# Scores and probability transposes of an attention group moved inside the next unit's projection, in a float32 two-block transformer kernel

## The chip, the cores and the metric

The kernel runs on one core of a Trainium2 chip. The metric is the device time of one execution in microseconds (us), lower is better. A profiled execution is one execution recorded by the hardware profiler; its trace gives for every instruction the engine, the start and the duration. TensorE is PE in the rows (PEld are its weight loads), VectorE is DVE, ScalarE is ACT, GpSimd is POOL, SyncE is SP.

## The reference

One sequence of 256 tokens by 1024 channels goes through two blocks in float32. The first is two layers: a multi-scale pooling mixer, and a differential attention of 8 heads, each followed by a gated feed-forward (1024 to 2816). The second is a token mixer with three branches (a block attention of 8 heads, a top-64 attention of 8 heads, a gated recurrence), followed by a squared-ReLU feed-forward (1024 to 4096). The attention parts, cut to what matters here:

```python
# differential attention, per head: two score maps of one head
s = einsum(q, k) * sm_scale + bias            # causal
p = softmax(s)
a = p[:, :, 0] - lam * p[:, :, 1]
o = einsum(a, v)

# the two attentions of the second block, per pair of heads
logits = einsum(q, k) * scale + bias (+ mask of the keys not chosen, second attention)
out = softmax(logits) @ v
```

## The kernel before

**Weights stream in units.** All weight matrices are cut into units of 128 x 2048 numbers (512 KB twice over). A unit is loaded by SP into one of three `raw` buffers, rounded by ScalarE into `w_hi` (line 1178, two instructions of 128x1024), and VectorE puts the rest, raw minus rounded, into `w_lo` (line 1190, two instructions). A product is then three fast matmuls: `w_hi` with the rounded activation, `w_hi` with the activation's rest, `w_lo` with the rounded activation (`three`, all recorded at line 525). A projection of one unit (`project`) is two column blocks of 8 such triples, 48 matmuls of 256 columns.

**The order is written out by hand.** Each engine has its own program, and semaphores link them. The units of the attention parts are: `U_HEAD` to `U_HEAD+7` (query and key of head 0 to 7, attention steps 0 to 7), `U_MOBA` to `U_MOBA+3` (steps 8 to 11, `A_MOBA` is 8), and `U_DSA` to `U_DSA+3` (steps 12 to 15, `A_DSA` is 12). These are the three attention groups. Two units `U_XC` follow the second group and two `U_YC` the third. A table of turns (`HEAD_TURNS`, `TURNS`) gives to each unit the step that is scored in its turn and the step that is applied in it: the step scored belongs to the unit before, the step applied to the unit two before. So in a group's second unit the group's first step is scored and nothing is applied; in its third unit the second step is scored and the first applied.

**One turn on TensorE, before:** `pe_turn_probs` (the transposes of the probabilities of the step that is applied, line 875; 3 in the first group, 6 in the others), then `pe_score` (the scores of the step that is scored: 4 float32 matmuls, recorded as 8), then the unit's projection, then `pe_apply` (the product with the values). `pe_score` waits for `proj_copied`: ScalarE must have copied the unit before from its PSUM bank into `qk` (line 1353). A unit's projection goes to bank 4, or to bank 5 where the unit is in `BANK5`.

**One turn on the others, first group** (loop over `HEAD_TURNS`): VectorE copies the transposed probabilities to SBUF (`v_prob_t`, line 1999, waits for `turned`), makes the logits (`v_logits`, line 1805, waits for `scored`), makes the rest of the unit two further on (`v_split`, line 1190), scales the exponentials to probabilities (`v_probs`, lines 1813 to 1822), and copies the output. ScalarE rounds the unit two further on, takes the exponentials (`s_softmax`, line 1318), copies the projected unit (line 1353), and sums squares.

**One turn on the others, second and third group** (`s_mixer`, `v_mixer`): here ScalarE begins the turn with the copy of the transposed probabilities (line 1373, waits for `turned`), and then rounds the unit two further on (line 1178), takes the exponentials (line 1318) and copies the projected unit (line 1353). VectorE makes logits (line 1805; in the third group with a mask added first, line 1798), the rest (line 1190), the probabilities (lines 1813, 1818), and then a piece of top-k or of a convolution and the rest of the output.

Of the kernel before, what the change touches and what calls it, by code (L numbers as in the profile page):

```python
# [25 lines left out]
KT = D // P  # L26
# [35 lines left out]
SLOTS = 3  # L62
# [6 lines left out]
U_HEAD = U_V + 4  # L69
# [3 lines left out]
U_QI = U_VA + 2  # L73
U_KI = U_QI + 2
U_VB = U_KI + 1
U_MOBA = U_VB + 2
U_XC = U_MOBA + 4
U_DSA = U_XC + 2
# [7 lines left out]
A_MOBA, A_DSA, A_END = 8, 12, 16  # L86
# [17 lines left out]
    return hi_place(unit)  # L104


BANK5 = (U_HEAD + 1, U_QI + 1, U_MOBA + 1)


def step_of(unit):  # L110
# [84 lines left out]
def build(nc, t, out):  # L195
    with ExitStack() as ctx:
# [3 lines left out]
        def sem(name):  # L200
            return ctx.enter_context(nc.semaphore(name))
# [11 lines left out]
        far_hi, far_lo = x_far[:, :, 0:SEQ], x_far[:, :, SEQ:2 * SEQ]  # L213
# [77 lines left out]
        lo_done = sem("lo_done")  # L291
        unit_done = sem("unit_done")
# [55 lines left out]
        v_copied = sem("v_copied")  # L348
# [9 lines left out]
        o_copied = sem("o_copied")  # L358
# [41 lines left out]
        def part(tile, slot, a):  # L400
            return tile[slot][:, :].rearrange("p (a b) -> p a b", a=a)
# [125 lines left out]
        def three(out_, w, w_rest, a, a_rest, start, stop):  # L527

            mm(out_, w, a, start=start, stop=False)
            mm(out_, w, a_rest, start=False, stop=False)  # L530
            return mm(out_, w_rest, a, start=False, stop=stop)
# [8 lines left out]
        def lo_part(slot, place, a):  # L540
            return lo_cells[slot][:, place:place + UW].rearrange("p (a b) -> p a b", a=a)

        def project(slot, outs, hi, lo, nk=KT, place=0):

            whi, wlo = part(w_hi, slot, nk), lo_part(slot, place, nk)
            for j, o in enumerate(outs):
                for k in range(nk):
                    c = slice(j * P, (j + 1) * P)
                    last = three(o, whi[:, k, c], wlo[:, k, c], hi[:, k, :], lo[:, k, :], k == 0, k == nk - 1)
            return last  # L550
# [305 lines left out]
        def proj_out(unit):  # L856
            return two5 if unit in BANK5 else two4

        def project_free(eng, unit):

            before = COPIED[unit] - (unit - 1 in BANK5)
            if before and unit not in BANK5:
                eng.wait_ge(proj_copied, before)

        def pe_turn_probs(eng, a):

            eng.wait_ge(prob_ready, a + 1)
            if 1 <= a <= A_MOBA:
                eng.wait_ge(pt_copied, a)
            elif a > A_MOBA:  # L870
                eng.wait_ge(pt_copied2, a - A_MOBA)
            for m in range(1 if a < A_MOBA else 2):
                for b in range(3):
                    c = slice(b * P, (b + 1) * P)
                    last = nc.tensor.transpose(bank[6 + m][:, c], prob[:, m, c], ident[:, :])  # L875
            last.then_inc(turned, 1)

        def pe_score(eng, a, unit):
            eng.wait_ge(proj_copied, COPIED[unit] + 1)
            if a >= 2:  # L880
                eng.wait_ge(logits_read, a - 1)
            if a == A_MOBA:
                eng.wait_ge(v_copied, 3)
                eng.wait_ge(dots_relu, 8)
            q_k = qk[a % 2]
            for m in range(2):
                s, r = bank[2 * (a % 2) + m], slice(m * DH, (m + 1) * DH)
                mm(s[:, 0:P], q_k[r, 0, 0:P], q_k[r, 1, 0:P], start=True, stop=True)
                last = mm(s[:, P:384], q_k[r, 0, P:SEQ], q_k[r, 1, 0:SEQ], start=True, stop=True)
            last.then_inc(scored, 1)  # L890

        def pe_apply(eng, a):
            if a < A_MOBA:
                eng.wait_ge(pt_copied, a + 1)
            else:
                eng.wait_ge(pt_copied2, a - A_MOBA + 1)
            if a >= 1:
                eng.wait_ge(o_copied, a)
            if a < A_MOBA:
                h = slice(a * VD, (a + 1) * VD)  # L900
                mm(bank[5][:, 0:P], prob_t[:, 0, 0:P], v1[:, 0, h], start=True, stop=True)
                mm(bank[5][:, P:SEQ], prob_t[:, 0, P:SEQ], v1[:, 0, h], start=True, stop=False)
                last = mm(bank[5][:, P:SEQ], prob_t[:, 0, SEQ:384], v1[:, 1, h], start=False, stop=True)
            else:
                v = v_a if a < A_DSA else v_b
                for m in range(2):
                    hd = 2 * ((a - A_MOBA) % 4) + m
                    o, h = bank[5][m * DH:(m + 1) * DH, :], slice(hd * DH, (hd + 1) * DH)
                    mm(o[:, 0:SEQ], v[:, 0, h], prob_t[:, m, 0:SEQ], start=True, stop=False)
                    last = mm(o[:, P:SEQ], v[:, 1, h], prob_t[:, m, SEQ:384], start=False, stop=True)  # L910
            last.then_inc(applied, 1)
# [45 lines left out]
        def pe_mixer(eng):  # L957
            score_unit = {step_of(u): u for u in range(U_QI, U_GATE)}
            for unit, apply, score_step in TURNS[2:]:
                if apply is not None:  # L960
                    pe_turn_probs(eng, apply)
                if score_step is not None:
                    pe_score(eng, score_step, score_unit[score_step])
                eng.wait_ge(lo_done, unit + 1)
                s = unit % SLOTS
                if unit in COPIED:
                    project_free(eng, unit)
                if unit == U_KI:
                    whi, wlo = (w[s][:, 0:KI_COLS * KT].rearrange("p (k c) -> p k c", k=KT) for w in (w_hi, w_lo))
                    for k in range(KT):  # L970
                        last = three(bank[4][0:KI_COLS, 0:SEQ], whi[:, k, :], wlo[:, k, :], far_hi[:, k, :],
                                     far_lo[:, k, :], k == 0, k == KT - 1)
                elif U_VB <= unit < U_MOBA:
                    j = unit - U_VB
                    if j == 0:
                        eng.wait_ge(v_copied, 2)
                    for i in range(NT):
                        last = rows(both_parts(unit, 4), [[bank[0][:, :]], [bank[1][:, :]]], far_hi, far_lo, 4 * j, 4, 512, j == 0, j == 1,
                                    (i,))
                        if i == 1:  # L980
                            last.then_inc(unit_done, 1)
                        if (i, j) == (0, 0):
                            eng.wait_ge(proj_copied, COPIED[U_KI] + 1)
                            for n in range(NT):
                                last = nc.tensor.transpose(bank[5][:, IDX_HEADS * n:IDX_HEADS * (n + 1)],
                                                           wi_t[:, n * P:(n + 1) * P], ident[DH:KI_COLS, DH:KI_COLS])
                            last.then_inc(wi_turned, 1)
                        pe_dots(eng, 2 * j + i)
                else:
                    last = project(s, proj_out(unit), far_hi, far_lo)  # L990
                if not U_VB <= unit < U_MOBA:
                    last.then_inc(unit_done, 1)
                if apply is not None:
                    pe_apply(eng, apply)
# [35 lines left out]
        def _(eng):  # L1030
# [79 lines left out]
                last.then_inc(psum_open, 1)  # L1110

            for unit, apply, score_step in HEAD_TURNS[:-1]:
                if apply is not None:
                    pe_turn_probs(eng, apply)
                if unit is None:
                    eng.wait_ge(x_ready, 4 * O_NORM + 1)
                    open_tile(0)
                if score_step is not None:
                    if score_step == 0:
                        eng.wait_ge(v_copied, 1)  # L1120
                    pe_score(eng, score_step, U_HEAD + score_step)
                if unit is not None:
                    eng.wait_ge(lo_done, unit + 1)
                    project_free(eng, unit)
                    project(unit % SLOTS, proj_out(unit), far_hi, far_lo).then_inc(unit_done, 1)
                if apply is not None:
                    pe_apply(eng, apply)
                if unit in (U_HEAD + 4, U_HEAD + 6):
                    pe_pair(eng, (unit - U_HEAD - 4) // 2)
# [206 lines left out]
        def s_copy_unit(eng, unit):  # L1336

            eng.wait_ge(unit_done, unit + 1)
            both = bank[5 if unit in BANK5 else 4][:, :].rearrange("p (a b) -> p a b", a=2)
            if unit == U_KI:  # L1340
# [883 lines left out]
```

## Time and profile before

| | us |
|---|---|
| three runs | 946.9, 947.38, 947.76 |
| median | 947.38 |
| the profiled execution | 947.05 |
| its span, first to last instruction | 945.2 |
| mean granted TensorE clock | 0.998 of full |

| engine | busy, us | share of the span |
|---|---|---|
| PE | 932.9 | 99% |
| PEld | 825.4 | 87% |
| DVE | 668.5 | 71% |
| ACT | 473.4 | 50% |
| POOL | 35.1 | 4% |

A busy time is the sum over instructions of one engine, overlaps counted once. The end of a matmul is modelled by the profiler, and matmuls overlap in the array; so the distance from one matmul's start to the next one's start tells what it costs, and the busy row tells only that TensorE hardly ever stands. The three attention groups lie at about 230 to 300, 547 to 591 and 591 to 636 us of the span.

### The profile page before, as it was taken

Reading aid. Unit: us, or ns where it says so; the run is one execution under the profiler, and the core shown is the slowest. Engines: PE = TensorE matmul, PEld = TensorE weight load, DVE = VectorE, ACT = ScalarE, POOL = GpSimd, SP = SyncE. Lnnn points to the kernel's source line nnn. Section 1 sums busy time; section 2 is a strip of 40 time slices with the busy share of each in tenths; the row PEclk is TensorE's granted clock in tenths of the full one; section 3 lists DMA queues with packets and bytes.
Section 4 is the critical chain, followed back from the end, with each engine's and each line's share of the span. In section 5 each row is a group of like instructions: output and inputs, shape, how many; then the busy total and the mean of one; then the engine's idle time right before and its main releaser. Section 6 shows DMA issues by size and latency. Waiting matters only on the chain.

```text
span 945.2 us, 15383 instructions
## 1 busy us (share of the span) xinstructions
PE 932.9 (99%) x5899; PEld 825.4 (87%) x5899; DVE 668.5 (71%) x964; ACT 473.4 (50%) x730; POOL 35.1 (4%) x63
## 2 busy tenths in 40 slices
PE   9999999999999999999999999999999999999997
PEld 7888888888898988888888889899999888888886
DVE  4776767676787887667678587976975666666663
ACT  4544444436666444444446556567754454434432
POOL 2010001000000000000001000000000000000000
PEclk9999999999999999999999999999999999999999
DMA  8586666639533387656554845544665536555531
GB/s 297 196 280 233 199 222 212 209 134 267 173 128 103 111 262 245 215 189 206 194 178 123 246 138 131 159 134 138 212 207 184 206 121 215 205 183 192 205 136 45
DMA packets 141648, 175.67 MB, mean 186 GB/s; under 512 B 7152, under 2 KB 119985, under 8 KB 141598
## 3 DMA queue, kind: packets, MB, share of 16 engines
q1 hardware_dynamic: 138384, 166.55, 54.7%
q0 software_dynamic: 2656, 8.31, 2.6%
q8 instruction: 34, 0.56, 0.3%
q10 hardware_dynamic: 558, 0.12, 0.1%
q14 instruction: 16, 0.13, 0.0%
HBM read 173.88 MB, written 1.09 MB: 185 GB/s over the span
## 4 chain that ended last, share of the span: by engine, by line
PE 90%; DVE 5%; ACT 2%; issue 1%; DMA 1%; POOL 0%; DVEq 0%; POOLq 0%; SPq 0%; ACTq 0%
PE bank L525 88%; DVE w_lo L1190 1%; PE bank L875 1%; PE bank L661 1%; ACT w_hi L1178 1%; DMA raw<-w_up 1%; DVE stats L1613 0%; DVE x_rows L1628 0%; DVE x_rows L1621 0%; DVE x_both L1600 0%; DVE arena L2059 0%; PE bank L673 0%; ACT arena L1318 0%; POOL rstd L2121 0%; ACT bank L1235 0%
## 5 line engine op out<-in xcount | busy, mean ns | idle before, releaser
L1190 DVE TENSOR_TENSOR w_lo<-raw,w_hi 128x1024 fp32r<-128x1024 f32 x308 | 362.6, 1220 | 85.4 <-ACT w_hi L1178 84.9
L525 PE MATMUL bank<-x_both,w_hi 128*128 128x256 f32 (+2 forms) x2050 | 409.5, 324 | 1.7 <-DVE w_lo L1190 0.9
L525 PEld LDWEIGHTS bank<-x_both,w_hi 128*128 128x128 f32 (+1 forms) x2050 | 339.7, 188 | 39.8 <-issue 6.4
L1178 ACT ACTIVATE w_hi<-raw 128x1024 fp32r<-128x1024 f32 x308 | 307.9, 1050 | 95.6 <-PE bank L525 85.1
L525 PE MATMUL bank<-x_both,w_lo 128*128 128x256 f32 (+1 forms) x1432 | 268.0, 277 | 0.0
L525 PEld LDWEIGHTS bank<-x_both,w_lo 128*128 128x128 f32 (+1 forms) x1432 | 212.8, 188 | 1.2
L525 PE MATMUL bank<-w_hi,arena_r 128*128 128x512 f32 x672 | 190.0, 391 | 0.2 <-DVE arena_r L1760 0.2
L525 PEld LDWEIGHTS bank<-w_hi,arena_r 128*128 128x128 f32 x672 | 124.5, 188 | 25.6 <-issue 1.2
L525 PE MATMUL bank<-w_lo,arena_r 128*128 128x512 f32 x336 | 106.2, 390 | 0.0
L1676 DVE TENSOR_REDUCE arena<-bank 128x512 f32<-128x1024 f32 x52 | 63.5, 1221 | 47.1 <-PE bank L525 47.1
L525 PE MATMUL bank<-w_hi,x_both 128*128 128x512 f32 (+1 forms) x352 | 77.4, 346 | 1.0 <-DVE x_both L1600 0.5
L525 PEld LDWEIGHTS bank<-w_lo,arena_r 128*128 128x128 f32 x336 | 63.1, 188 | 13.2
L525 PEld LDWEIGHTS bank<-w_hi,x_both 128*128 128x128 f32 x352 | 55.4, 188 | 10.1 <-issue 1.8
L1249 ACT ACTIVATE arena<-arena 128x512 f32<-128x512 f32 x20 | 12.6, 632 | 81.4 <-DVE arena L1676 81.4
L525 PE MATMUL bank<-arena 64*128 64x256 f32 (+7 forms) x346 | 49.0, 351 | 3.2 <-ACT arena L1353 2.2
L1260 ACT ACTIVATE arena_r<-arena 128x512 fp32r<-128x512 f32 x20 | 12.7, 634 | 67.1 <-PE bank L525 61.3
L525 PEld LDWEIGHTS bank<-arena 64*128 64x128 f32 (+2 forms) x346 | 33.6, 186 | 12.4 <-issue 5.9
L525 PE MATMUL bank<-w_lo,x_both 128*128 128x512 f32 (+1 forms) x176 | 41.4, 341 | 0.1
L1353 ACT ACTIVATE arena<-bank 128x512 f32<-128x512 f32 x22 | 13.1, 597 | 49.6 <-PE bank L525 49.6
L1287 ACT ACTIVATE arena_r<-arena 128x512 fp32r<-128x512 f32 x15 | 9.5, 634 | 48.5 <-PE bank L525 47.7
L1709 DVE TENSOR_TENSOR arena_r<-arena,arena_r 128x512 fp32r<-128x512 f32 x20 | 13.8, 691 | 27.1 <-ACT arena_r L1260 27.1
L525 PE MATMUL bank<-arena_r,w_hi 128*128 128x256 f32 x192 | 32.9, 276 | 0.0
(179 smaller groups left out, 602.4 us busy)
## 6 DMA issues: line engine op xcount, KB each, us to landing
raw<-w_up SPq DMA_DIRECT2D x76, 512.0 KB, 4.5
raw<-w_down SPq DMA_DIRECT2D x76, 512.0 KB, 4.2
raw<-w_in SPq DMA_DIRECT2D x60, 512.0 KB, 4.6
raw<-w_gate SPq DMA_DIRECT2D x44, 512.0 KB, 4.8
raw<-w_qkv SPq DMA_DIRECT2D x24, 512.0 KB, 4.8
raw<-w_o SPq DMA_DIRECT2D x16, 512.0 KB, 4.2
table<-bias_vectors POOLq DMA_DIRECT2D x12, 256.0 KB, 4.6
raw<-w_pa SPq DMA_DIRECT2D x4, 512.0 KB, 4.5
```

The lines of the kernel that those rows point to most:

```text
L525: return nc.tensor.matmul(*a, skip_group_check=True, **k)
L661: last = nc.tensor.transpose(b[:, k * P:(k + 1) * P], src[:, i, (4 * h + k) * P:(4 * h + k + 1) * P], ident[:, :])
L875: last = nc.tensor.transpose(bank[6 + m][:, c], prob[:, m, c], ident[:, :])
L1178: nc.scalar.activation(hi_cells[slot][:, to], raw[slot][:, c], ACT.Copy).then_inc(hi_done, 1)
L1190: last = nc.vector.tensor_tensor(lo_cells[slot][:, place + c.start:place + c.stop], raw[slot][:, c], hi_cells[slot][:, hi_at + c.start:hi_ ...
L1249: nc.scalar.activation(ffn_e.rearrange("p (a b) -> p a b", a=2), gate_sum, ACT.Tanh, scale=0.5).then_inc(tanh_done, 1)
L1260: nc.scalar.activation(h_hi[buf], hidden_rows, ACT.Copy).then_inc(h_rounded, 1)
L1287: nc.scalar.activation(h_hi[buf], hidden_rows, ACT.Copy).then_inc(m_rounded, 1)
L1353: nc.scalar.activation(dst, both, ACT.Copy).then_inc(proj_copied, 1)
L1676: return V.tensor_reduce(o, banks8[:, b:b + 2, :].rearrange("p a (h t) -> p a t h", h=2), mybir.AxisListType.X, ALU.add)
L1709: V.tensor_tensor(h_lo[buf], ffn_h.rearrange("p (a b) -> p a b", a=2), h_hi[buf].bitcast(F32), ALU.subtract).then_inc(h_ready, 1)
```

## The change

In the second and the third turn of each of the three groups TensorE's order changes. The second turn (score of the group's first step, nothing applied) starts with the projection; after the first three triples of its first column block (9 matmuls) come the scores. The third turn (score of the group's second step, first step applied) starts with the projection too; the scores stand after 9 matmuls, and the probability transposes of the group's first step, which stood ahead of everything, now stand between the two column blocks, after 24 matmuls and the scores. `U_DSA+1` is added to `BANK5`, with a wait for `o_copied` before its projection, and so goes to the bank beside that of `U_DSA`; `U_HEAD+1` and `U_MOBA+1` were there already. The programs of VectorE, ScalarE, GpSimd and SyncE are not edited, and no DMA is moved.

```diff
-BANK5 = (U_HEAD + 1, U_QI + 1, U_MOBA + 1)
+BANK5 = (U_HEAD + 1, U_QI + 1, U_MOBA + 1, U_DSA + 1)
+SCORED_INSIDE = (0, 1, A_MOBA, A_MOBA + 1, A_DSA, A_DSA + 1)
...
-        def project(slot, outs, hi, lo, nk=KT, place=0):
+        def project(slot, outs, hi, lo, nk=KT, place=0, between={}):
...
                 for k in range(nk):
+                    if (j, k) in between:
+                        between[j, k]()
...
+        def inside(eng, unit, apply, score_step):
+
+            eng.wait_ge(lo_done, unit + 1)
+            project_free(eng, unit)
+            if apply is None and score_step:
+                eng.wait_ge(o_copied, score_step)
+            between = {(0, 3): lambda: pe_score(eng, score_step, unit - 1)}
+            if apply is not None:
+                between[1, 0] = lambda: pe_turn_probs(eng, apply)
+            return project(unit % SLOTS, proj_out(unit), far_hi, far_lo, between=between)
...
             for unit, apply, score_step in TURNS[2:]:
+                if score_step in SCORED_INSIDE:
+                    assert score_unit[score_step] == unit - 1
+                    inside(eng, unit, apply, score_step).then_inc(unit_done, 1)
+                    if apply is not None:
+                        pe_apply(eng, apply)
+                    continue
...
             for unit, apply, score_step in HEAD_TURNS[:-1]:
+                if score_step in SCORED_INSIDE:
+                    if score_step == 0:
+                        eng.wait_ge(v_copied, 1)
+                    inside(eng, unit, apply, score_step).then_inc(unit_done, 1)
+                    if apply is not None:
+                        pe_apply(eng, apply)
+                    continue
```

TensorE's order in the first group, before, from the end of the projection of `U_HEAD+1` to the start of that of `U_HEAD+2`. Projection matmuls read `x_both` and `w_hi` or `w_lo`, the transposes read `ident`, the scores only `arena`:

```order
L525 MATMUL bank<-x_both,w_lo 128x256
L875 MATMUL bank<-ident,arena 128x128 [waits prob_ready]
L875 MATMUL bank<-ident,arena 128x128 x2
L525 MATMUL bank<-arena 128x128 [waits proj_copied]
L525 MATMUL bank<-arena 128x256
L525 MATMUL bank<-arena 128x128
L525 MATMUL bank<-arena 128x256
L525 MATMUL bank<-x_both,w_hi 128x256 [waits proj_copied,lo_done]
L525 MATMUL bank<-x_both,w_hi 128x256
L525 MATMUL bank<-x_both,w_lo 128x256
```

The same engine in the changed kernel, the scores inside the first column block of `U_HEAD+2`:

```order
L526 MATMUL bank<-x_both,w_lo 128x256
L526 MATMUL bank<-arena 128x128 [waits proj_copied]
L526 MATMUL bank<-arena 128x256
L526 MATMUL bank<-arena 128x128
L526 MATMUL bank<-arena 128x256
L526 MATMUL bank<-x_both,w_hi 128x256 x2
```

And the transposes in the changed kernel, after the 24th projection matmul of `U_HEAD+2`:

```order
L526 MATMUL bank<-x_both,w_hi 128x256 x2
L526 MATMUL bank<-x_both,w_lo 128x256
L889 MATMUL bank<-ident,arena 128x128 [waits prob_ready]
L889 MATMUL bank<-ident,arena 128x128 x2
L526 MATMUL bank<-x_both,w_hi 128x256 x2
```

The scores have moved behind 9 projection matmuls and the transposes behind 24 and the scores.

ScalarE's order in the third turn of the second group (`U_MOBA+2`), before, from the copy of the transposed probabilities of step 8 to the exponentials of step 9:

```order
L1373 ACTIVATE arena<-bank 128x384 [waits turned]
L1373 ACTIVATE arena<-bank 128x384
L1178 ACTIVATE w_hi<-raw 128x1024 [waits unit_done,raw_in0]
L1178 ACTIVATE w_hi<-raw 128x1024
L1318 ACTIVATE arena,zsum<-arena,nmax 128x128 [waits prob_ready,logits_read]
```

The same place in the changed kernel:

```order
L1398 ACTIVATE arena<-bank 128x384 [waits turned]
L1398 ACTIVATE arena<-bank 128x384
L1203 ACTIVATE w_hi<-raw 128x1024 [waits unit_done,raw_in0]
L1203 ACTIVATE w_hi<-raw 128x1024
L1343 ACTIVATE arena,zsum<-arena,nmax 128x128 [waits prob_ready,logits_read]
```

On ScalarE nothing has moved but the line numbers; what has moved is the event that its first row waits for. VectorE's order is the same in both kernels too.

## Rows read from the trace of the kernel before

**Rows 1.** The page, busy time of TensorE: us, share of span, instructions.

```profile
PE 932.9 (99%) x5899; PEld 825.4 (87%) x5899; DVE 668.5 (71%) x964; ACT 473.4 (50%) x730; POOL 35.1 (4%) x63
```

**Rows 2.** TensorE's waits, whole span: us in total, times, longest.

```profile
PE bank L525 <- ACT arena L1353: 2.2, 3, 0.8
```

**Rows 3.** Timeline, first group: start, us, engine, line, operation, count [idle before].

```profile
235.87 0.28 PE L525 MATMUL bank<-x_both,w_lo 128*128 128x256 f32 x1
236.19 0.60 ACT L1353 ACTIVATE arena<-bank 128x512 f32<-128x512 f32 x1 [1.70 <-PE bank L525]
236.93 0.93 PE L525 MATMUL bank<-arena 64*128 64x128 f32 x8 [0.78 <-ACT arena L1353]
237.79 0.50 PE L525 MATMUL bank<-x_both,w_hi 128*128 128x256 f32 x2
...
243.25 0.28 PE L525 MATMUL bank<-x_both,w_lo 128*128 128x256 f32 x1
243.76 0.55 PE L875 MATMUL bank<-ident,arena 128*128 128x128 f32 x3 [0.23 <-DVE arena L1822]
...
251.33 0.49 PE L875 MATMUL bank<-ident,arena 128*128 128x128 f32 x3
```

**Rows 4.** Timeline, first group, VectorE: copy, logits, rest, reciprocal.

```profile
241.90 0.18 DVE L1813 RECIPROCAL rz<-zsum 128x4 f32<-128x4 f32 x1 [0.53 <-ACT arena L1318]
...
244.34 0.56 DVE L1999 COPY arena<-bank 128x384 f32<-128x384 f32 x1 [0.64 <-PE bank L875]
245.23 0.29 DVE L1805 CUSTOM_DVE_ANT_0 arena<-bank,table 128x128 f32<-128x128 f32 x1 [0.33 <-PE bank L525]
...
246.34 2.36 DVE L1190 TENSOR_TENSOR w_lo<-raw,w_hi 128x1024 fp32r<-128x1024 f32 x2
...
248.62 0.17 DVE L1813 RECIPROCAL rz<-zsum 128x4 f32<-128x4 f32 x1
```

**Rows 5.** Timeline, second group: TensorE, ScalarE and VectorE.

```profile
553.60 0.93 PE L525 MATMUL bank<-arena 64*128 64x128 f32 x8 [0.69 <-ACT arena L1353]
...
558.76 0.17 DVE L1813 RECIPROCAL rz<-zsum 128x4 f32<-128x4 f32 x1
...
560.03 0.88 PE L875 MATMUL bank<-ident,arena 128*128 128x128 f32 x6
...
560.94 0.87 ACT L1373 ACTIVATE arena<-bank 128x384 f32<-128x384 f32 x2
561.70 2.01 ACT L1178 ACTIVATE w_hi<-raw 128x1024 fp32r<-128x1024 f32 x2
...
563.60 0.40 ACT L1318 ACTIVATE arena<-arena,nmax 128x128 f32<-128x128 f32 x1
...
565.48 0.18 DVE L1813 RECIPROCAL rz<-zsum 128x4 f32<-128x4 f32 x1
...
567.38 0.88 PE L525 MATMUL bank<-arena 128*64 128x256 f32 x8
568.18 0.87 PE L875 MATMUL bank<-ident,arena 128*128 128x128 f32 x6
```

**Rows 6.** Timeline, third group, TensorE.

```profile
598.13 0.93 PE L525 MATMUL bank<-arena 64*128 64x128 f32 x8 [0.69 <-ACT arena L1353]
...
604.92 0.88 PE L875 MATMUL bank<-ident,arena 128*128 128x128 f32 x6 [0.20 <-DVE arena L1818]
...
613.25 0.88 PE L875 MATMUL bank<-ident,arena 128*128 128x128 f32 x6
```

**Rows 7.** Timeline, TensorE: transposes with a projection right behind them.

```profile
629.70 0.88 PE L875 MATMUL bank<-ident,arena 128*128 128x128 f32 x6
630.33 0.48 PE L525 MATMUL bank<-x_both,w_hi 128*128 128x256 f32 x2
```

**Rows 8.** Stretches at the end: length, PE, PEld, DVE, ACT, POOL, PEclk, DMA.

```profile
939.00:940.00 1.00, 0.61 (x3) 0.19 (x1) 0.00 (x0) 0.35 (x1) 0.00 (x0) 1.00 0.00 0
...
942.00:942.20 0.20, 0.00 (x0) 0.00 (x0) 0.20 (x2) 0.00 (x0) 0.00 (x0) 0.50 0.00 0
```

More of the change, by code:

```diff
@@ L1118, in _ @@
                 if score_step is not None:
-                    if score_step == 0:
-                        eng.wait_ge(v_copied, 1)
                     pe_score(eng, score_step, U_HEAD + score_step)
```

## The prediction

> **What bounds the kernel now.** I read the page first. TensorE is busy for 932.9 of the 945.2 us span [rows 1], so time is won only where TensorE stands or where its instructions are too far apart. The view of waits comes next, for TensorE alone: the projections' line waited three times for ScalarE's copy of a projected unit, 2.2 us in total [rows 2]. These are the scores of the first step of each group. The timeline then shows each place from start to start, which is the true cost since the ends are modelled. In the first group a projection's last matmul starts at 235.87; at 0.12 a matmul the next could start at 235.99. The copy runs from 236.19 to 236.79, the scores start at 236.93: 0.94 us lost [rows 3]. The row itself shows 0.78 of idle, by modelled ends; so 0.16 is to be added to such a bracket. In the second and third group the scores have a bracket of 0.69 [rows 5, 6], which makes 0.85 each: projections that end at 552.75 and 597.28, and scores at 553.60 and 598.13. The group's first transposes can wait too: the last matmul starts at 243.25 and they at 243.76, so 0.39 is lost [rows 3]; 0.0 in the second group [rows 5], and 0.20 + 0.16 = 0.36 in the third [rows 6]. All that the change can take away is thus 0.94 + 2 x 0.85 + 0.39 + 0.36 = 3.4 us.
>
> **What moves, and what it costs by itself.** Nothing is added or removed. From 237.79 to 243.25 lie 47 matmul starts, so a projection matmul costs 0.116 and one unit 5.58; the scores in front of it cost 0.86 [rows 3]. Scores and projection together are 6.44, wherever in it the scores stand. For the transposes with a projection behind them the price is 0.63 for six (629.70 to 630.33) [rows 7], which is less than what they take in front of scores. One more change between kinds of matmul per group costs at most the 0.11 by which the first matmul behind scores is longer; I take 0.11, so 0.3 in all. The scores at their new place find their copy done: 9 matmuls from 235.99 end at 237.03, the copy at 236.79. That is a margin of 0.24; where it fails, the scores stand for a few tenths. The bank added for `U_DSA+1` holds the output of a step whose copy lies a whole projection back, so I price its wait at nothing; if that cover were gone it would give back the third 0.85.
>
> **The wait that appears.** Who waits for the transposes? In the second and third group ScalarE's turn begins with their copy, and behind this copy, in order, stand the rounding of a weight unit and the exponentials of the next step. In the first group VectorE waits with its copy, and behind it stand the logits, the rest of a weight unit, and the probabilities. These orders do not change, only the transposes come later; and TensorE's next transposes need those probabilities. So I follow the chain from transposes to transposes.
>
> Second group, from the rows of step 8 [rows 5]: transposes to copy 0.91 (560.03 to 560.94), copy to rounding 0.76, rounding to exponentials 1.90, exponentials to VectorE's reciprocal 1.88 (563.60 to 565.48), reciprocal to transposes 1.27 (558.76 to 560.03). Together 6.72. Before, TensorE needed 8.15 (560.03 to 568.18) for the same turn, so the chain was hidden with 1.4 to spare. In the changed kernel TensorE has only the transposes (0.63), 24 matmuls (2.78) and the value product (0.80, 567.38 to 568.18, and about 0.1 ahead of it) behind the moved transposes: 4.31. It must stand 6.72 - 4.31 = 2.4 us for the probabilities of step 9.
>
> The sum goes from the end of the group's first projection to the second transposes, since behind them all is again in the old order and phase:
> - Second group: start 552.75; unit two 6.43 (553.60 to 560.03, scores and projection), to 559.18; unit three up to the transposes 9 x 0.116 + 0.86 + 15 x 0.116 + 0.11 = 3.75, to 562.93; chain 6.72, to 569.65. Before: 568.18 [rows 5]. Later by 1.47.
> - Third group: start 597.28; 6.43 + 3.75 + 6.72 = 16.90, to 614.18. Before: 613.25 [rows 6]. Later by 0.93; less, since before lost 0.36 more here. VectorE has more to do for logits in this group, but the scores come early enough for that.
> - First group, on VectorE [rows 3, 4]: start 235.99; 6.44 and 3.75, transposes at 246.18. Chain: 0.58 to the copy (243.76 to 244.34), the copy 0.56, logits 1.11 (245.23 to 246.34), rest 2.28 (246.34 to 248.62), reciprocal to transposes 1.86 (241.90 to 243.76): 6.39, to 252.57. Before: 251.33. Later by 1.24. The exponentials run beside the rest and are the shorter of the two.
>
> Sum: 1.47 + 0.93 + 1.24 = +3.64 us. So 3.4 are won and about 7.1 given back (three stands of 2 to 2.5 us). After the second transposes of a group TensorE's turn is again longer than the chain (8.15 against 6.72), so the delay does not grow, and since TensorE has no slack behind it, it reaches the end whole. The profiled execution took 947.05, 0.33 under the median; 947.05 + 3.64 = 950.7, and by the median 951.0. Bounds for the unknown parts: each of the three chains can be read 0.4 too long or too short by semaphore times and by overlapping copies, and the switch of kinds may cost nothing or twice: 949.3 to 952.6.
>
> **The clock.** New here are stands of TensorE of up to 2.4 us; the longest before in an attention group is 0.78 [rows 3]. At the very end TensorE's last matmul ends at about 939.61, and from 942.0 on the granted clock is 0.50, the 1.2 GHz level, 2.4 us after it [rows 8]. So a stand of this length is on the edge of what the trace shows to be followed by the low level. The Trainium skill ("TensorE: Matmul & The Clock Gate", section "Why this matters for your kernels") warns against idle gaps between bursts of matmuls, since the clock then falls back to half. [...] That no stand in an attention group of before was as long leaves it open here.
>
> **Rivals.**
> - *Faster, 944.3 us (7 in 100).* The probabilities of the second step are there when TensorE asks. Then all 3.4 us are kept, less 0.3 for the switches: 947.38 - 3.4 + 0.3. For it speaks that TensorE is the bound and that its waits are real. It decides at a chain of 4.3 us in place of 6.72, and against that stands every row of the chain, each of which is in the engine's own order.
> - *Within noise, 947.2 us (9 in 100).* The chain is shorter in the last two groups by the 1.90 of the rounding, as if the exponentials did not queue behind it: 951.0 - 2 x 1.90. Against it: the exponentials start at 563.60, at the rounding's end, though the logits had been ready [rows 5]. The Trainium skill ("Perfetto Trace Analysis", section "Tensor Engine Instruction (MATMUL, LD_WEIGHTS)") says that ScalarE and VectorE queues are strictly in order. With that rule the time is 951.0, without it 947.2; the trace agrees with it.
> - *Much slower (12 in 100).* The granted clock falls in one or more of the stands. The price of one fall is unknown below one projection at half speed, 5.58 more, and above nothing; I take half, 2.8: 953.8 for one, and more for several.
> - *Chain as read, 951.0 us (72 in 100).*
>
> **How the numbers follow.** The predicted time is 951.0. The range takes in the bounds of the sum and one fall of the clock, 949.1 to 953.8; left out are the two faster cases and a piece of the slowest. A measurement of this kernel can tell about 0.2% from no change, which is 1.9 us: faster below 945.5 has 0.07, within has 0.11 (the second rival, and a sum that is 1.7 too large), slower above 949.3 has 0.82.
>
> **What would show it.** In the profile of the changed kernel: no wait of TensorE for the copy of a projected unit in the groups (right for 2.2 us gained). The first transposes of each group without a wait in front, and the second transposes with the longest idle of TensorE in an attention group, 1.8 to 2.6 us, put down to VectorE's probabilities. ScalarE idle ahead of its copy of transposed probabilities in the third turn for some 3 us. Third transposes of each group without a wait. If the second transposes wait for less than a microsecond, the chain was read wrongly; if TensorE's clock is under 1.00 behind a stand, the third rival holds; if the scores show an idle of more than 0.3 ahead of them, the margin of the copy was too thin.

## The result, and the profile after

| | before | changed kernel |
|---|---|---|
| median, us | 947.14 | 954.72 |
| single executions, us | 946.54 to 947.76 | 951.57, 953.97, 955.47, 955.68 |
| mean granted clock of these | 0.998 (profiled one) | 0.997, 0.996, 0.994, 0.994 |
| the profiled execution, us | 947.05 | 951.57 |
| its span, us | 945.2 | 949.8 |

The ratio is 1.0077 (95% interval 1.0065 to 1.0089): slower, as forecast, but by twice what was forecast, and above the range. The profiled execution is the fastest of the four, and the slower they are the lower is their clock. That is to be kept in mind with every row below: this profile shows less than the median lost.

The page's busy line, against [rows 1]:

```profile
PE 933.5 (98%) x5899; PEld 826.3 (87%) x5899; DVE 668.8 (70%) x964; ACT 472.6 (50%) x730; POOL 34.5 (4%) x63
```

The same 5899 matmuls are busy for 0.6 us more by their modelled ends, the span is 4.6 longer: nearly all of it is standing still.

TensorE's waits, whole span of the changed kernel (us in total, times, longest), against [rows 2]:

```profile
PE bank L889 <- DVE arena L1843: 4.4, 2, 2.2
PE bank L889 <- DVE arena L1847: 2.3, 1, 2.3
```

The three waits for the copy of a projected unit, 2.2 us, are gone. In their place are three waits of the transposes (line 889) for VectorE's probabilities, 6.7 us, the longest 2.3.

The timeline of the changed kernel, TensorE's scores and transposes of each group, against [rows 3, 5, 6] (start, us, operation, count, idle before):

```profile
236.27 0.93 PE L526 MATMUL bank<-arena 64*128 64x128 f32 x8
...
251.72 0.55 PE L889 MATMUL bank<-ident,arena 128*128 128x128 f32 x3 [2.35 <-DVE arena L1847]
...
554.25 0.93 PE L526 MATMUL bank<-arena 64*128 64x128 f32 x8
560.77 0.93 PE L526 MATMUL bank<-arena 64*128 64x128 f32 x8
563.45 0.81 PE L889 MATMUL bank<-ident,arena 128*128 128x128 f32 x6
...
570.12 0.88 PE L889 MATMUL bank<-ident,arena 128*128 128x128 f32 x6 [2.22 <-DVE arena L1843]
...
600.33 0.93 PE L526 MATMUL bank<-arena 64*128 64x128 f32 x8
...
616.20 1.39 PE L889 MATMUL bank<-ident,arena 128*128 128x128 f32 x6 [2.21 <-DVE arena L1843]
```

From a group's first scores to its second transposes it takes 15.45, 15.87 and 15.87 us. The sum of the prediction has 15.54, 15.86 and 15.86 (from 237.03 to 252.57, from 553.79 to 569.65, from 598.32 to 614.18). And the chain that makes the stand of the second group, on ScalarE and VectorE of the changed kernel, against [rows 5]:

```profile
564.30 0.87 ACT L1398 ACTIVATE arena<-bank 128x384 f32<-128x384 f32 x2 [3.85 <-PE bank L889]
565.06 2.01 ACT L1203 ACTIVATE w_hi<-raw 128x1024 fp32r<-128x1024 f32 x2
...
566.96 0.40 ACT L1343 ACTIVATE arena<-arena,nmax 128x128 f32<-128x128 f32 x1
...
568.84 0.18 DVE L1838 RECIPROCAL rz<-zsum 128x4 f32<-128x4 f32 x1 [0.33 <-ACT arena L1343]
```

ScalarE idles 3.85 us for the moved transposes (563.45), where some 3 were forecast; then copy, rounding, exponentials and probabilities follow one upon another, and the next transposes start at 570.12, 6.67 us after the first.

What the sum did not have is in the last row of the timeline: six transposes there take 1.39 and not 0.88. The stretches of that place (length, PE, PEld, DVE, ACT, POOL, PEclk, DMA share, GB/s) show the granted clock:

```profile
616.00:616.40 0.40, 0.20 (x2) 0.20 (x3) 0.40 (x2) 0.00 (x0) 0.00 (x0) 1.00 0.74 159
616.40:616.80 0.40, 0.40 (x4) 0.40 (x3) 0.36 (x2) 0.00 (x0) 0.00 (x0) 0.51 0.96 317
...
619.20:619.60 0.40, 0.40 (x2) 0.40 (x3) 0.36 (x1) 0.40 (x2) 0.00 (x0) 0.50 0.02 5
619.60:620.00 0.40, 0.40 (x5) 0.40 (x4) 0.40 (x2) 0.40 (x1) 0.00 (x0) 0.73 0.00 0
620.00:620.40 0.40, 0.40 (x6) 0.40 (x5) 0.37 (x2) 0.39 (x1) 0.00 (x0) 1.00 0.00 0
```

TensorE is back at work from 616.20 on, and the clock falls to the 1.2 GHz level at 616.4, behind a stand of 2.2 us, and is back at 2.4 GHz 3.4 us later.

### The profile page after: what moved, and what is told of

The parts are those of the page before. It is cut to its first block, busy times and chain, and to the rows that moved or that the text cites. A ratio compares the mean times of both kernels' runs of the same rounds, so it can differ in the third digit from the quotient of the medians.

```text
span 949.8 us, 15384 instructions
## 1 busy us (share of the span) xinstructions
PE 933.5 (98%) x5899; PEld 826.3 (87%) x5899; DVE 668.8 (70%) x964; ACT 472.6 (50%) x730; POOL 34.5 (4%) x63
## 4 chain that ended last, share of the span: by engine, by line
PE 91%; DVE 5%; ACT 2%; issue 1%; DMA 1%; POOL 0%; DVEq 0%; POOLq 0%; SPq 0%; ACTq 0%
PE bank L526 89%; DVE w_lo L1215 1%; PE bank L889 1%; ACT w_hi L1203 1%; PE bank L664 1%; DMA raw<-w_up 1%; DVE stats L1638 0%; DVE x_rows L1653 0%; DVE x_rows L1646 0%; DVE x_both L1625 0%; ACT arena L1343 0%; DVE arena L1843 0%; DVE arena L2084 0%; PE bank L676 0%; ACT bank L1260 0%
```

## The experiments

The theory: two costs, one on top of the other. The moved transposes delay a chain on the other engines (this gives some 950.4), and the stands that this makes let TensorE's clock fall, in some executions more often than in others. The rival: the part above 950.7 has another source, such as DMA or longer chains.

**The change again, and with TensorE kept busy in its stands.** The second kernel adds nine small matmuls without a use where TensorE would stand. `keep_warm` multiplies the identity with itself into a bank whose content nobody needs; the kernel before already calls it at other places, around its norms, but not in the attention groups:

```diff
                     if apply is not None:
                         pe_apply(eng, apply)
+                        keep_warm(bank[6], 9)
                     continue
```

> The changed kernel as it is, timed again beside the runs below. The chain theory alone gives 950.7 to 951.0. The clock theory says that each of the three stands of TensorE of 2.2 to 2.4 us can be followed by a stretch of some 3.3 us at half clock that costs about 1.6 us, so that single executions lie at 950 + 1.6 x (0, 1, 2 or 3), the median at 953 to 955, and the mean granted clock falls as the time rises.

> The changed kernel with 9 small matmuls without a use (18 records, some 2 us) behind the value product of each third turn, where TensorE stands for the probabilities. The stand is the same length for the rest of the work, only TensorE is kept busy in it. Clock theory: no half-speed stretch in the three groups, all executions within 1 us of each other, median 950.0 to 950.8, that is 3 to 4.5 us under the changed kernel. A rival, that the extra over the chain comes from DMA or ScalarE and not from the clock: same time as the changed kernel, 953 to 955, or a little more.

The change again: 954.94 us (five executions, 952.06 to 955.86), ratio 1.0077. With TensorE kept busy: 950.42 us (950.12 to 950.54), ratio 1.0036 (1.0022 to 1.0049), clock 0.998 or 0.999 in each of the five. The spread falls from 3.8 to 0.4 us. Its timeline in the second group:

```profile
568.49 2.27 PE L526 MATMUL bank<-ident 128*128 128x128 f32 x18
570.78 0.88 PE L889 MATMUL bank<-ident,arena 128*128 128x128 f32 x6
```

The real work is not a bit earlier (the transposes follow the first ones at 564.11 by 6.67 us, as in the changed kernel), the stand is only filled. So the 4.5 us between 950.4 and 954.9 go with TensorE's standing and the falls of its clock, and what is left, 950.42 against 946.95 before, 3.5 us, is the chain. The profiled execution of the change again, which took 954.94, shows the fall in the first group:

```profile
250.00:252.00 2.00, 0.00 (x0) 0.00 (x0) 1.89 (x7) 0.63 (x3) 0.00 (x0) 1.00 0.11 26
252.00:254.00 2.00, 1.70 (x9) 1.37 (x11) 1.14 (x3) 1.39 (x5) 0.00 (x0) 0.51 1.03 301
254.00:256.00 2.00, 2.00 (x10) 1.35 (x9) 1.15 (x9) 1.20 (x2) 0.00 (x0) 0.50 0.81 197
256.00:258.00 2.00, 2.00 (x11) 2.00 (x11) 2.00 (x4) 1.86 (x8) 0.00 (x0) 0.50 0.00 0
...
258.00:258.50 0.50, 0.50 (x4) 0.50 (x3) 0.47 (x3) 0.00 (x0) 0.00 (x0) 0.50 0.00 0
258.50:259.00 0.50, 0.50 (x5) 0.50 (x4) 0.46 (x3) 0.00 (x0) 0.00 (x0) 0.64 0.00 0
```

Here the low level lasted 6.8 us, twice as long as in the other profile, and the turn from the second transposes to the third took 10.58 us (252.30 to 262.88). Without a fall it took 7.55 in the changed kernel's other profile (251.72 to 259.27) and 7.77 in the kernel kept busy, so the fall cost 2.8 to 3.0. In its third group the low level lasted 3.4 us and the turn took 9.72 in place of 8.32, 1.4 more; in the second group there was no fall. Taking these costs off brings this execution to 950.5 to 950.7, and taking 1.4 off the first profile (951.57) gives 950.2: both land on the kernel kept busy, so the falls account for all of the extra. A stand of 2.2 to 2.35 us is followed by nothing, by one such stretch, or by two.

**Each half of the change.** The first kernel keeps the scores of a group's first step inside the projection, and leaves the third turn as it was before (the change of bank for `U_DSA+1` stays):

```diff
-SCORED_INSIDE = (0, 1, A_MOBA, A_MOBA + 1, A_DSA, A_DSA + 1)
+SCORED_INSIDE = (0, A_MOBA, A_DSA)
```

> Only the second turn of each group is changed (scores of the group's first step inside the projection); the third turn stands as before. The 2.2 us of waits for the projected copy are gone. If a wait removed were a gain: 944.5. Chain theory: the probabilities of the first step are not ready earlier (ScalarE's and VectorE's own work sets them), so TensorE stands for them at the third turn as much longer as it was saved: transposes at the same time, no change, 946.8 to 947.6, with three waits for VectorE's probabilities of 0.8 to 1.2 us each.

947.19 us (ten executions, 946.38 to 948.08), ratio 1.0003 (0.9993 to 1.0012): no change. Its waits of TensorE:

```profile
PE bank L889 <- DVE arena L1843: 1.8, 2, 1.2
PE bank L889 <- DVE arena L1847: 1.0, 1, 1.0
```

The three waits of 2.2 us in total are gone, and 2.8 stand in front of the transposes (0.61, 1.05 and 1.20), where before there were 0.4. The wait for the copy was no loss of its own: it lay beside a chain on ScalarE and VectorE that ended later. In the second group the new wait is 0.61, a little under the 0.8 expected.

The second kernel is the whole change, but the transposes of the third turn stand 9 projection matmuls in, right ahead of the scores:

```diff
+            def early():
+                pe_turn_probs(eng, apply)
+                pe_score(eng, score_step, unit - 1)
+
             between = {(0, 3): lambda: pe_score(eng, score_step, unit - 1)}
             if apply is not None:
-                between[1, 0] = lambda: pe_turn_probs(eng, apply)
+                between = {(0, 3): early}
```

> The changed kernel, but in the third turn of each group the transposes stand after 9 projection matmuls, right ahead of the scores, 1.7 to 2.7 us earlier than in the change. Chain theory: they come just when the probabilities are ready, the chain of 6.7 us to the next transposes is then as long as TensorE's own work, so nearly no stand is left: 944.8, between 944.0 and 945.6, clock at full in the groups. If the place of the transposes did not matter: as the changed kernel, 951 to 955.

944.02 us (six executions, 943.78 to 944.42), ratio 0.9969 (0.9957 to 0.9981): faster than before, 0.8 under the 944.8 expected and at the lower end of the range given. The timeline of its second group:

```profile
558.62 0.82 PE L893 MATMUL bank<-ident,arena 128*128 128x128 f32 x6
559.37 0.93 PE L526 MATMUL bank<-arena 64*128 64x128 f32 x8
...
565.66 0.87 PE L893 MATMUL bank<-ident,arena 128*128 128x128 f32 x6
```

No wait stands in front of either transposes of this group; 7.04 us lie between them, more than the 6.67 of the chain. The list of waits has for the probabilities only this row; both waits are in the third group (0.18 and 0.19), where the distance is 7.52, because there VectorE makes the masked logits only by 606.7 and the exponentials wait for them:

```profile
PE bank L893 <- DVE arena L1847: 0.4, 2, 0.2
```

So the scores may stand inside the projection, and the transposes too: 9 projection matmuls in, the two moves together gain 2.9 us, where the first alone gained nothing. What made the change slow is how far back the transposes went.

**How far back, in two steps.** The place of the transposes, `(1, 0)` in the change, moved 6 projection matmuls earlier and 9 later:

```diff
-                between[1, 0] = lambda: pe_turn_probs(eng, apply)
+                between[0, 6] = lambda: pe_turn_probs(eng, apply)
```

> The changed kernel with the transposes of each third turn 6 projection matmuls (0.70 us) earlier. Chain theory: the second transposes follow 0.70 us earlier in each group, the stand shrinks from 2.2 to 1.5 us: 950.4 (the changed kernel with TensorE kept busy) less 2.1, 948.3 without falls of the clock. Clock theory: with the shorter stand fewer or no half-speed stretches, so the median is at 948.3 to 949.5 and the spread of single executions under 2 us. If the falls depend only on there being a stand, the median is 4.5 above, 952.8.

```diff
-                between[1, 0] = lambda: pe_turn_probs(eng, apply)
+                between[1, 3] = lambda: pe_turn_probs(eng, apply)
```

> The changed kernel with the transposes of each third turn 9 projection matmuls (1.05 us) later. Chain theory: stands of 3.3 us, 950.4 + 3.1 = 953.5 without falls. Clock theory: a fall in nearly every stand, each costing 1.6 to 2.5: median 958.5 to 961, mean granted clock at or under 0.994.

Earlier: 948.92 us (eleven executions, 947.93 to 950.88), ratio 1.0022. The rows of its waits, all three shorter by 0.7:

```profile
PE bank L889 <- DVE arena L1843: 3.0, 2, 1.5
PE bank L889 <- DVE arena L1847: 1.7, 1, 1.7
```

The lowest, 947.93, is at what the chain alone gives (948.3). Three of the eleven, 950.34 to 950.88, had a clock of 0.996 or 0.997; the profiled one (950.88) shows a low stretch of 3.4 us in the first group, behind the 1.66 us stand. The median is inside the 948.3 to 949.5 expected, but the spread is 2.95 us where I had expected under 2: a stand of 1.7 can still be followed by a fall. Nor is all of the spread the clock's. The eight others lie from 947.93 to 949.85, and the last of these has a clock of 0.999; what makes these 1.9 us the runs don't show.

Later: 957.89 us (four executions, 957.18 to 958.79), ratio 1.0114, clock 0.992 to 0.994 in all. Its waits:

```profile
PE bank L889 <- DVE arena L1843: 6.5, 2, 3.3
PE bank L889 <- DVE arena L1847: 3.4, 1, 3.4
```

In its profile the low level stands once behind each of the three stands, 3.4 us each time. 953.5 for the chain and three falls of 1.4 to 1.6 are 957.7 to 958.3. The 958.5 to 961 expected missed: they had a fall too dear, at 1.6 to 2.5 us.

**One group alone.**

```diff
-SCORED_INSIDE = (0, 1, A_MOBA, A_MOBA + 1, A_DSA, A_DSA + 1)
+SCORED_INSIDE = (A_DSA, A_DSA + 1)
```

> The change in the third group alone; the first and second stand as before. Chain theory: +0.93 on 947.0, 947.9 without a fall. With one fall in most executions: 949.5, single executions in two clusters 1.6 us apart. If the three groups did not add up (say all the loss in the first), no change.

948.16 us (eleven executions), ratio 1.0016 (1.0007 to 1.0025). Six executions lie from 947.57 to 948.16 with a clock of 0.999, four from 949.21 to 949.95 with 0.997. The median of the six, 947.61, is 0.7 over before for 0.93 in the sum; that of the four, 949.48, is 1.9 above it. So by time and clock four of the eleven had a fall; where in the kernel it came, an execution without a profile doesn't tell. The eleventh is the profiled one, 949.06 with 0.998. Its third group shows the stand, and no low clock in this group:

```profile
615.42 0.88 PE L889 MATMUL bank<-ident,arena 128*128 128x128 f32 x6 [2.22 <-DVE arena L1843]
```

It had its fall elsewhere, at the kernel's start, where TensorE waited 1.1 us for a DMA. The rows are the transpose and the 36 small matmuls behind that wait:

```profile
11.77 0.22 PE L1076 MATMUL bank<-ident,arena 33*128 33x33 f32 x1 [1.11 <-DMA arena<-subln_g]
11.91 9.92 PE L526 MATMUL bank<-arena 33*24 33x384 f32 x36
```

The granted clock in this place (length, PE, PEld, DVE, ACT, POOL, PEclk, DMA share, GB/s):

```profile
12.00:14.00 2.00, 2.00 (x9) 1.25 (x10) 1.11 (x1) 0.97 (x4) 0.00 (x0) 1.00 1.04 378
14.00:16.00 2.00, 2.00 (x7) 1.60 (x6) 0.30 (x1) 0.00 (x0) 0.00 (x0) 0.53 1.10 346
16.00:18.00 2.00, 2.00 (x7) 1.61 (x6) 0.40 (x1) 0.98 (x2) 0.00 (x0) 0.61 1.11 350
```

The same 36 matmuls in the kernel before:

```profile
12.11 8.23 PE L525 MATMUL bank<-arena 33*24 33x384 f32 x36
```

The 36 take 1.7 us longer, which puts this execution without its fall at 947.4, beside the six. So a fall can come outside the groups, behind a stand of 1.1 us and when TensorE had been at work again for over 2 us, and it could have been so in the four too. Against that speak the 63 executions of kernels in which TensorE never stands over 1.2 us in the groups (42 of the kernel before, 10 with the first half of the change, 6 with the transposes 9 matmuls in, 5 with TensorE kept busy): none is more than 0.9 us over its kernel's median, where a fall costs 1.4 or more. That the 2.2 us stand caused the four is therefore likely, but not shown.

**The bank.**

```diff
-BANK5 = (U_HEAD + 1, U_QI + 1, U_MOBA + 1, U_DSA + 1)
+BANK5 = (U_HEAD + 1, U_QI + 1, U_MOBA + 1)
```

> The changed kernel without its change of bank for the second unit of the third group, which then waits 0.85 us for the copy ahead of its projection, as its scores did before. Chain theory: the third group's whole chain starts 0.85 later, so 0.85 over the changed kernel, 955.8 by the median. If the stand swallowed it (slack in the chain): as the changed kernel, 954.9.

954.31 us (four executions, 953.92 to 955.51) looks like the changed kernel's 954.94, and the expectation of 955.8 like a miss. The median misleads here: the profiled execution (953.92) has one fall alone, in the second group, where the turn took 9.70 us in place of 8.33. Without it that execution would be at 952.5, which is 2.1 over the change without falls (950.42). Its timeline shows why it is more than the 0.85 expected; the other bank saved a wait at two units, `U_DSA+1` and the one behind it. For the first the profile names no releaser, but ScalarE's copy ends at 602.00, just ahead of it:

```profile
601.09 0.28 PE L526 MATMUL bank<-x_both,w_lo 128*128 128x256 f32 x1
602.10 0.47 PE L526 MATMUL bank<-x_both,w_hi 128*128 128x256 f32 x2 [0.73 <-issue]
...
608.58 0.28 PE L526 MATMUL bank<-x_both,w_lo 128*128 128x256 f32 x1
609.63 0.47 PE L526 MATMUL bank<-x_both,w_hi 128*128 128x256 f32 x2 [0.78 <-ACT arena L1378]
```

At 0.11 a matmul, 0.90 and 0.94 us are lost there, 1.8 of the 2.1; the rest is within the spread of single executions. That four executions of this kernel had fewer falls than those of the change may be chance; the runs don't tell.

## Why the prediction was right or wrong

**Right: what bounds the kernel, what is gained, and the chain.** The waits for the projected copy went, the scores found their copy (no idle ahead of them), the second transposes have the longest idle of an attention group (2.2 to 2.35 us for a forecast of 1.8 to 2.6), and the third transposes have none. The sum of +3.64 us, 950.7 by the profiled execution and 951.0 by the median, is measured at 950.42 where the clock is held up, +3.5 on the kernel before. That is no luck: each group's own distance came out within 0.1 us.

**Right: which rivals would not come.** No faster case came. The second rival, exponentials that need not queue behind the rounding, is refuted by the changed kernel's own rows: ScalarE starts them at 566.96, at the end of the rounding, though the logits were made by 563.05.

**Wrong: the clock as a rival of 12 in 100.** This is the step that failed. I read from [rows 8] that the clock falls 2.4 us after TensorE's last matmul, saw that the new stands are 2.0 to 2.5 us long, and called that an edge. But the sum held the falls at nothing, the rival was one chance for three stands together, and the range put one fall on the middle of the sum, not on its upper bound (952.6 + 2.8 would be 955.4). Measured, the falls are 4.5 us, more than the chain. All nine executions of the changed kernel are above 951.5 with a mean clock of 0.994 to 0.997, where the kernel kept busy is never above 950.54, so each had at least one fall. Even the four in eleven of the kernel with one group, taken for a stand's chance, would leave one execution in four without a fall ((7/11) cubed), and would make about one fall an execution, 1.5 to 2 us and not 4.5. Whether the first group's stand, a little longer at 2.35 us, is the likelier one, or one fall makes the next likelier, the runs leave open. Either way the case that I called a rival was the likeliest one.

Nor was one row enough to read an edge from. At the end of the ten profiles the clock falls from 2.2 to 4.4 us after the last matmul's end (3.4 in the changed kernel), and in the groups it fell seven times out of eight when TensorE was already at work again, 0.2 to 1.8 us after the stand. How long TensorE stands is thus not all that decides. The Trainium skill ("TensorE: Matmul & The Clock Gate", section "Why this matters for your kernels") warns of idle gaps between bursts of matmuls, but of longer ones than the stands of this kernel; by it alone no fall was due. The trace differs, with falls behind 2.21 and 2.34 us, and decides.

**Wrong in size: a fall's price.** The prediction took 2.8 us, between nothing and 5.58. A stretch of 3.4 us at the low level costs 1.4 to 1.9 us: 1.4 by the turns of the second profile, 1.7 at the start of the kernel with one group, 1.9 by the two clusters of that kernel. It is not 3.4, because TensorE does half of the work in it. Only the double stretch of the first group cost 2.8 to 3.0; that this is the figure I took for a single one is chance. Mean number and price make the gap: 954.9 - 950.4 = 4.5 us, three single stretches or what is worth as much.

**Not said: the gain of 3.4 us was never there to be had by moving the scores alone.** The prediction counted the waits for the copy as gained and the stands as given back. The kernel with the first half alone shows that these 2.2 us are covered by the chain of the probabilities. They are won only if the transposes come as soon as the probabilities are there and TensorE has projection matmuls to do until then, as in the kernel at 944.02. The first rival's time, 944.3, was thus within reach, but by another place of the transposes.

**The bank's cover.** The prediction priced the loss of it at 0.85; it is 1.8, since a second unit waits too. It did not enter the sum.

## What to carry to other kernels

A wait on the busiest engine is worth only what the chain behind the next wait leaves of it; follow that chain on the other engines before the wait is counted as a gain. When a producer step is moved back on an engine that others wait for, sum their queue from this step to the next thing that comes back, and place the step where that sum just fits (in the second group here 7.0 us of TensorE's work against 6.7; 944.02 in place of 954.94). And count a stand of TensorE of some 2 us at its length plus the chance of a low clock behind it, 1.4 to 1.9 us a time here, and let the range hold as many falls as there are stands.

## What the runs showed of the hardware

- The granted clock can fall behind a stand of 1.7 to 2.4 us, once behind one of 1.1 (at 14.1 for work from 11.77 on), and mostly when TensorE is at work again: at 616.4 for work from 616.20 on. The low level then lasted 3.4 us, once 6.8, in every profile with a fall. With three stands of 1.5 to 1.7 us an execution a low mean clock came in three of eleven, with one of 2.2 us in four of eleven, and with three of 3.3 us in all four, in the profile once behind each stand. Where in an execution without a profile the fall came is not known.
- Eighteen matmul records of no use in each stand of some 2.2 us held the clock at full in all five executions, and took the median from 954.94 to 950.42. For a stand that can't be removed it is the only cure tried here.
- Transposes with a projection on either side cost less than in front of scores: six take 0.57 us from start to start (563.45 to 564.02), in front of scores 0.81 (570.12 to 570.93). And 2.68 us lie from the scores at 560.77 to the transposes at 563.45 against 2.71 in the sum, so the change of kinds of matmul is within the 0.11 taken for it.
